# Expert gathers issued slot by slot instead of in blocks of four: a PEER layer on one core

## What is computed

```python
def peer_block(x, w_query, sub_keys, expert_u, expert_v):
    ...
    experts = jnp.take_along_axis(cidx, pos, axis=-1)      # 8 heads x 16 experts per token
    g = jax.nn.softmax(top_s, axis=-1)
    u = expert_u[experts]
    v = expert_v[experts]
    a = jax.nn.gelu(jnp.einsum('td,thkd->thk', x, u).astype(jnp.float32), approximate=False)
    return jnp.einsum('thk,thkd->td', (g * a).astype(x.dtype), v)
```

## Time and profile before

| | us |
|---|---|
| median of 3 runs | 3503.11 (3503.08 to 3503.35) |
| the profiled execution's own time | 3499.09 |
| its span | 3497.3 |
| PE busy | 2499.0 (71%) |
| POOL busy | 2290.4 (65%) |
| DVE busy | 2279.7 (65%) |
| ACT busy | 812.6 (23%) |

### The profile page before, as it was taken

One profiled execution on the slowest core, in us unless ns is written; L12 is line 12 of the kernel. 1 busy time (PEld: TensorE's weight loads), 2 busy tenths in 40 slices (PEclk: granted clock), 3 DMA queues, 4 the chain that ended last, 5 costly groups with the idle time before them and its releaser, 6 DMA issues.

```text
span 3497.3 us, 38783 instructions
## 1 busy us (share of the span) xinstructions
PE 2499.0 (71%) x11520; PEld 1392.1 (40%) x11520; DVE 2279.7 (65%) x5456; ACT 812.6 (23%) x2057; POOL 2290.4 (65%) x2068
## 2 busy tenths in 40 slices
PE   7558775878764598777744978778656978776764
PEld 6425442645531264445311644445213534332321
DVE  3585586655688756657898466558796455554774
ACT  2112212232211212322112223322112122221111
POOL 0366575655657776676777767666676676657675
PEclk8779887999987799899877999889876798987777
DMA  6699999988999999999999999999999999999998
GB/s 237 224 399 363 347 410 334 388 313 298 372 351 372 370 404 371 352 366 412 409 371 372 397 392 349 331 374 410 405 371 379 388 387 370 368 323 394 411 409 338
DMA packets 368936, 1279.47 MB, mean 366 GB/s; under 512 B 59372, under 2 KB 77974, under 8 KB 353368
## 3 DMA queue, kind: packets, MB, share of 16 engines
q0 software_dynamic: 297216, 1082.26, 80.7%
q1 hardware_dynamic: 62324, 168.67, 12.6%
q10 hardware_dynamic: 9188, 26.05, 2.3%
HBM read 1262.31 MB, written 13.48 MB: 365 GB/s over the span
## 4 chain that ended last, share of the span: by engine, by line
DVE 37%; PE 30%; DMA 15%; issue 8%; ACT 4%; SPq 3%; POOL 2%; DVEq 0%; ACTq 0%; POOLq 0%
DVE u_ring L1736 15%; PE acc L924 9%; PE front L586 8%; DMA u_ring<-in_expert_u,pick_cur 7%; DMA v_ring<-in_expert_v,pick_cur 4%; PE front L802 3%; DVE si_u L1603 2%; SPq L536 2%; DVE sv L1602 2%; PE front L711 2%; DVE work L1603 2%; DMA w_ukT<-in_cache_krope 2%; POOL u_ring L1853 1%; DVE work L1602 1%; PE front L734 1%
## 5 line engine op out<-in xcount | busy, mean ns | idle before, releaser
L924 PE MATMUL acc<-v_ring,diag 128*64 128x512 f32 x4096 | 1161.5, 716 | 612.6 <-ACT diag L1222 352.9
L1853 POOL DMA_INDIRECT v_ring<-in_expert_v,pick_cur x1024 | 1133.2, 1107 | 606.1 <-PE acc L924 333.0
L1853 POOL DMA_INDIRECT u_ring<-in_expert_u,pick_cur x1024 | 1140.5, 1114 | 575.4 <-issue 295.1
L1736 DVE CUSTOM_DVE_ANT_0 u_ring<-u_ring,xn_cur 128x1024 f32<-128x1024 f32 x1024 | 1210.8, 1222 | 315.4 <-DMA u_ring<-in_expert_u,pick_cur 309.3
L924 PEld LDWEIGHTS acc<-v_ring,diag 128*64 128x64 f32 x4096 | 340.7, 163 | 1316.6 <-issue 856.9
L1222 ACT ACTIVATE diag<-ident,wgt 128x64 f32<-128x64 f32 x1024 | 272.3, 337 | 797.6 <-DVE wgt L1742 727.9
L586 PE MATMUL front<-work,w_ring 128*128 128x256 f32 (+2 forms) x1536 | 308.1, 343 | 31.0 <-DVE mo L1337 17.1
L586 PE MATMUL front<-mo,w_ring 128*128 128x256 f32 (+2 forms) x1536 | 300.5, 337 | 0.0
L586 PEld LDWEIGHTS front<-work,w_ring 128*128 128x128 f32 x1536 | 250.5, 200 | 83.0 <-issue 29.3
L1215 ACT ACTIVATE gelu<-dots 128x4 f32<-128x4 f32 x256 | 52.5, 205 | 962.9 <-DVE dots L1736 962.8
L586 PEld LDWEIGHTS front<-mo,w_ring 128*128 128x128 f32 x1536 | 255.3, 201 | 23.4
(11 more groups left out here) (303 smaller groups left out, 2374.6 us busy)
## 6 DMA issues: line engine op xcount, KB each, us to landing
w_ring<-in_w_pieces SPq DMA_DIRECT2D x112, 1024.0 KB, 8.4
u_ring<-in_expert_u,pick_cur POOLq DMA_INDIRECT x1024, 10.5
v_ring<-in_expert_v,pick_cur POOLq DMA_INDIRECT x1024, 9.7
x_t<-in_x_prompt SPq DMA_DIRECT2D x16, 512.0 KB
v_ring<-in_w_pieces SPq DMA_DIRECT2D x8, 1024.0 KB, 12.0
work<-in_cache_ckv SPq DMA_DIRECT2D x64, 128.0 KB, 7.9
xn_cur<-scratch ACTq DMA_DIRECT2D x14, 512.0 KB, 9.8
scratch_x<-rows_next ACTq DMA_DIRECT2D x8, 512.0 KB, 6.6
```

Of the source, the lines that this page charges most:

```text
L924: last = nc.tensor.matmul(acc[rows, half, :], diag[:, s % RING, :], v_ring[:, s % RING, half * 512:half * 512 + 512], start=(s < 2), stop= ...
L1736: v.tensor_tensor_reduce(u_ring[:, slot, :], u_ring[:, slot, :], xn2_cur[:, block_of(r), :], 1.0, 0.0, ALU.mult, ALU.add, dots[:, g * G + ...
L1853: pool.indirect_dma_start(ring[:, slot, :], None, a[table][0], bass.IndirectOffsetOnAxis(ap=pick, axis=0)).then_inc(loaded[slot], 16)
```

## The change

`gather_group` is taken apart into `picks_ready`, `gather_u` and `gather_v`. For each group g of a tile but the last, POOL now issues u of slot s + 4, v of slot s, u of slot s + 5, v of slot s + 1 and so on, where it issued four of u and then four of v. For each slot the wait, the table, the place in the ring and the semaphore are as before. The number of gathers is the same.

```diff
-            def gather_group(it, g, table, ring, loaded):
+            def picks_ready(it, g):
                 u, i = unit_of(it)
                 for part, (h0, h1) in enumerate(parts_of(u)):
                     if g * G == h0 * TOPK:

                         pool.wait_ge(on.picks_moved, selected(u, part, i))
-                if it == 0 and g == 0 and table == "expert_v":
-                    pool.wait_ge(on.w_used, START_PIECES)
-                for s in range(g * G, (g + 1) * G):
-
-                    if table == "expert_u":
-                        pool.wait_ge(on.u_free, it * SLOTS + s + 1)
-                    else:
-                        pool.wait_ge(on.v_free, it * SLOTS + s + 1)
-                    waited(pool)
-                    gather(table, ring, s % RING, loaded, pick_bufs[it % PICK_BUFS][:, s:s + 1])
+
+            def gather_u(it, s):
+
+                pool.wait_ge(on.u_free, it * SLOTS + s + 1)
+                waited(pool)
+                gather("expert_u", u_ring, s % RING, u_loaded, pick_bufs[it % PICK_BUFS][:, s:s + 1])
+
+            def gather_v(it, s):
+
+                pool.wait_ge(on.v_free, it * SLOTS + s + 1)
+                waited(pool)
+                gather("expert_v", v_ring, s % RING, v_loaded, pick_bufs[it % PICK_BUFS][:, s:s + 1])

             for it in range(TILES):
-                gather_group(it, 0, "expert_u", u_ring, u_loaded)
+                picks_ready(it, 0)
+                for s in range(G):
+                    gather_u(it, s)
                 for g in range(GROUPS):
+                    if it == 0 and g == 0:
+                        pool.wait_ge(on.w_used, START_PIECES)
                     if g + 1 < GROUPS:
-                        gather_group(it, g + 1, "expert_u", u_ring, u_loaded)
-                    gather_group(it, g, "expert_v", v_ring, v_loaded)
+                        picks_ready(it, g + 1)
+                    for s in range(g * G, (g + 1) * G):
+                        if g + 1 < GROUPS:
+                            gather_u(it, s + G)
+                        gather_v(it, s)
```

## The result

| | before | after |
|---|---|---|
| median, lowest to highest (6 runs each), us | 3503.22 (3502.58 to 3510.40) | 3650.58 (3643.82 to 3663.07) |
| the profiled execution, us | 3499.09 | 3653.74 |
| its span, us | 3497.3 | 3651.9 |
| POOL, DVE, PE busy, us | 2290.4, 2279.7, 2499.0 | 2269.6, 2285.0, 2530.4 |

The changed kernel is slower: ratio 1.0419 (1.0399 to 1.0439), +147 us. The forecast was 3596 us, in a range of 3500 to 3680.

A forecast was written before the change was run, and what follows sets the result against it. The loop was taken as tied by two rings and four in-order lists, its end moving with POOL's waits and gather lengths. Terms 0 + 93 + 0 + 0 = +93 us on 3503.1 gave 3596 us, range 3500 to 3680.

The forecast's parts named there:

- POOL's account: POOL's gather time, pauses and real waits sum to 3329 us of loop; the end moves with its waits and gather lengths.
- 1.24 us for each gather: An undisturbed gather costs POOL 0.94 + 0.30 us; the example stall's last u goes out at 1258.0 instead of 1243.03.
- 25 runs x 3.72 us = 93 us: Runs of groups where DVE waits for u, less four starting a tile, each pay three gathers' delay once: +93 us.
- Both countings: Two estimates of the loss from late u: 80 us by share of groups without slack, 93 us by runs of groups.
- The upper bound of 286 us: All 77 POOL stalls for v each pass their full 3.72 us to the end.
- What v gains: PE gets a group's first v pair 2.48 us earlier, but its fourth v keeps its place: gain taken as 0.
- rival 2: PE's earlier first v pair frees places sooner and shortens POOL's stalls: faster, 3462 us; chance 0.07.
- The length of the gathers: POOL's gathers are stretched by DVE's dot products, 355 us in all; the number of dots stays, so 0 change.
- Rival 3: Spread DVE dots each meet another POOL gather and lengthen it: 77 us on top of the 93, 3673 us; chance 0.10.
- w_used: The wait for w_used moves some 7 us earlier, ahead of the second u group; cost 0, at most 7 us once.
- Rival 1: The loop is bound by DMA bandwidth, so gather order is of no account: 3503 us; chance 0.10.
- Rival 4: Each of the 77 POOL stalls for v lets 3.72 us through, no slack left: 3789 us; chance 0.05.

The follow-up runs named there:

- e7: Kernel before, with the change's order only in the 179 groups where POOL did not stall for v, blocks in the other 77: 3600.4 us, ratio 1.0278.
- e6: Kernel before, with the change's order only in the 77 groups whose first v stalled in the old trace, blocks elsewhere: 3570.3 us, ratio 1.0207.
- e9: Change's order with half rows for v and 12 v places: 3421.5 us, ratio 0.9771 to kernel before; its partner, same with old block order, 3375.8 us.
- e11: Change's order with half rows for v and 8 v places: 3534.1 us, ratio 1.0101 to kernel before; the same with old block order, 3398.0 us.
- the ladder: Orders with 0 to 4 u rows of a group put behind its first v, against the kernel before: ratios 1, 1.0049, 1.0211, 1.0448, 1.0558.

## Why the prediction was right in kind and short in size

**POOL's account** closes: real waiting 425 to 601, +176; busy 2290.4 to 2269.6, -21; together +155 us, and the span grew by 154.6. It is bookkeeping, though. An engine's time is always its work, its pauses and its waits, so the account says where the time lies and not why.

**1.24 us for each gather** held, and so did the example. The last u of the stalled group goes out 6.2 us after the end of the stall (1298.49 to 1304.70), as 1251.81 + 5 x 1.24 = 1258.0 had it, and lands after the time at which DVE used to need it.

**The size is where it failed.** The term "25 runs x 3.72 us = 93 us" should have read 147. Both countings looked only at places where the old trace already waits: the 77 stalls and the 72 groups in which DVE waits for u. (The 115 waits lie in 70 groups and 31 runs, so the term was 27 x 3.72 = 100 us.) The change makes new stalls: from 77 to 115 and from 283 to 517 us. Of the 52 new ones 34 arise where the place of the first v had been free for less than 3.72 us, which could be worked out from the old trace and was not looked for. e7 bears it out: +102 us from groups that had no stall to lengthen, with 204 us of new ones.

That 93 came so near is in part luck. The term prices groups in which DVE waits for u, while the loss was argued from stalls for v, and these are mostly not the same groups: only 21 of the 70 have their u rows ahead of a stalled v. e6 (72 us) therefore doesn't confirm the 93. Whether a run pays its delay only once stays open. The falling behind is even, some 0.6 us for each group (147 / 256), and that doesn't tell the two countings apart. The upper bound of 286 us was never near, and it priced 7 stalls in last groups of a tile, where the order stays; without them it is 260.

**What v gains, 0**, was not measured by itself. PE's waits for v did fall, from 259.2 to 154.4 us. But its waits for diag rose by more, from 352.9 to 508.0 us, as they would where PE comes earlier to the next wait, for a weight that DVE makes later. The kernel is slower, so rival 2 falls as a forecast; that nothing at all of its gain reached the end is argued, not shown.

**The length of the gathers, 0**, was right: the means went from 1107 and 1114 to 1099 and 1102 ns. Rival 3 needed POOL's busy time to rise by about 80 us, and it fell by 21. The rule behind it (the Trainium skill, GPSIMD Engine Reference, Key points: GpSimd contends with VectorE instructions that read two SBUF inputs) fits both traces. Before, 888 gathers overlap a dot product and hold 334 of the 355 us of stretching; after, 1024 gathers do and hold 316. So spread dots do meet more gathers, as the rival said, but each stretches less (0.31 us in the mean, where it was 0.38), and the sum doesn't rise. Only in e9, where hardly anything stalls, is POOL busy for 26 us more than in its partner.

**w_used, 0**, was right. The first gathers of the changed kernel, beside the earlier trace rows, have the first v in the sixth place with the plain pause ahead of it:

```profile
134.84 1.37 POOL L1853 DMA_INDIRECT u_ring<-in_expert_u,pick_cur  x1 [0.30 <-issue]
136.52 1.92 POOL L1853 DMA_INDIRECT v_ring<-in_expert_v,pick_cur  x1 [0.30 <-issue]
```

**Rival 1** (a DMA-bound loop) is excluded by the time, by e11 and by the queue itself, which got shorter. The tile's rows of u, beside the earlier trace rows, keep their duration:

```profile
L1853 POOL DMA_INDIRECT u_ring<-in_expert_u,pick_cur x1024: 933/938/3443, 129.7 to 3600.1; - x171
```

and the median from issue to landing fell from 10.5 to 8.8 us for u and from 9.7 to 8.1 for v, so the queue that a gather meets is shorter, and the DMA engines stand idle more. In the stretches of the earlier trace rows the share of the DMA engines went from 0.95 to 0.91 in the first, and from 0.98 to 0.95 in the second:

```profile
131.00:1000.00 869.00, 604.61 (x2921) 374.64 (x2923) 549.01 (x1341) 200.78 (x490) 503.80 (x465) 0.85 0.91 341
1000.00:2000.00 1000.00, 650.47 (x2634) 340.26 (x2632) 715.17 (x1762) 220.11 (x573) 664.86 (x612) 0.82 0.95 359
```

**Rival 4** (3789 us) wasn't reached.

**The signs.** POOL's waits for u on DVE fell (138.9 to 82.5), DVE's for u passed 450 (602.5), those before the second to fourth dot appeared (52 to 508 us together), the DMA share fell below 0.97 but for the last stretch (0.99), and POOL's busy time kept within 30 us. One sign missed: the waits for v were to rise by 100 to 200 us and rose by 233. That is the same under-count as in the sum.

**Open.** How the 147 us divide between "later" and "further apart" is bounded only with half rows: 90 of 136 go with the stalls, and the spacing, the two tables, longer gathers and the few stalls left share the other 46. With whole rows more places weren't tried, nor were more places for u. No order that was run is faster than the old one.

## What to carry to other kernels

Where one in-order queue feeds two rings, put the gathers whose places are surely free ahead of those that may have to wait; each row that is put behind a stalling gather is paid for, also in places that do not stall yet. When you price such a move, don't count only the waits that the old trace shows: a gather that moves forward makes a new stall wherever its place was free by less than the move. Count these near misses too; here 52 groups stalled anew, for 136 us. The time that an engine stands in a stall is not its price: 197 us of stalls were worth 22 us in one order, 340 us were worth 113 in the other. To see which part of a loss is the stall, give the ring more places and run both orders again.

## What the runs showed of the hardware

- The gathers land in the order of their issue, one every 1.28 us in the median of the kernel before. The four v rows issued from 1251.81 us on the earlier trace rows, for one, landed from 1261.23 to 1265.01, 1.26 us apart; alternating, u rows land 2.54 us apart (1304.80 to 1312.43). For 524 KB, 1.28 us is 410 GB/s. The Trainium skill (DMA: Bandwidth & Descriptors, Anatomy of one DMA) gives a slope of 436 GB/s and 2.0 us fixed, about 3.2 us for one alone by our estimate. The pace agrees with the slope within 6%. The shortest from issue to landing here is 4.6 us for u and 4.2 for v, more than 3.2; with other transfers under way in these traces, that doesn't tell whether the fixed part is larger.
- An indirect gather's issue is stretched where it overlaps dot products: the 1160 of 2048 that overlap none take 0.02 us over the 0.937 in the mean, the 888 that do 0.38 us, and one beside four of them took 4.71 us (at 1258.01 us of the kernel before).
- The granted TensorE clock is a little lower where PE waits more: 0.87 to 0.85 in the first stretch, 0.84 to 0.82 from 1000 to 2000 us; from 3000 us on it is not (0.81 and 0.82). One matmul of the v groups takes 725 ns for 716, which is 22 us of PE's busy time in 4096. How much of it reaches the end wasn't separated.
- On one occasion the kernel before took 3613.8 us instead of 3500, and spread over 38 us instead of 8 to 21. What made it slower isn't known; the order of the four kernels run there is the same as the ladder's elsewhere.
